# Norm of the mixing input by tokens with x turned on TensorE, a new order around the first gathers, and a gather ring of six slots with one weight unit kept on chip

## The reference, cut to what matters

```python
def layer(x, ret_state, conv_buf, ...):          # x: 1024 prompt frames + 32 sample frames, 1024 wide
    h = rmsnorm(x, g_mix)                        # over each token's 1024 numbers
    q, k, v, g, gb, gc, hc = split(h @ w_in)     # w_in 1024 x 3584: 2048 columns q,k,v,g, then 1536 of the conv
    o = retention(rotary(q), rotary(k), v)       # 4 heads x 128, state carried on from chunk to chunk
    o = rms_scale(o) * silu(g)
    c = gb * short_conv(gc * hc)
    x = x + concat([o, c]) @ w_out
    x = x + peer(rmsnorm(x, g_ffn), wq, keys1, keys2, u_tab, v_tab)
    return rmsnorm(x, g_final)

def peer(x, ...):                                # per token: 8 heads, 16 experts each
    q = (x @ wq).reshape(.., 8, 2, 128)
    ...                                          # top 16 of 128 + 128 keys, top 16 of the 256 pairs
    act = gelu(einsum('td,thkd->thk', x, u_tab[eidx]))
    return einsum('thk,thkd->td', gate * act, v_tab[eidx])
```

## Time and profile before

| | |
|---|---|
| median of 3 runs | 3058.72 us (3057.13 to 3068.32) |
| the profiled execution, its own time | 3063.58 us |
| its span in the trace | 3061.8 us |
| first gather issued | at 135.17 us of the span |
| last gather issued | at 3032.74 us of the span |
| bytes moved by DMA | 1228.73 MB |

### The profile page before, as it was taken

How to read it: one execution, slowest core, us unless ns; L and a number is a source line. 1 busy time by engine, 2 the same in 40 slices (tenths; PEclk the granted TensorE clock), 3 DMA queues, 4 the chain that set the end, 5 groups by cost and what they waited for, 6 DMA issues and landing times.

```text
span 3061.8 us, 36499 instructions
## 1 busy us (share of the span) xinstructions
PE 2305.2 (75%) x12780; PEld 1879.1 (61%) x12780; DVE 2066.9 (68%) x5094; ACT 2035.8 (66%) x3700; POOL 1223.2 (40%) x1060
## 2 busy tenths in 40 slices
PE   8977887787677887877666787888777775667766
PEld 6766677665566775755555666665556555555554
DVE  2365887666688775666888844566578899954454
ACT  1177766667677666776676766667766777676665
POOL 0033333344433333443333344334434444555653
PEclk9988999888888989888888989989987887666666
DMA  7499999999999999999999999999999999999997
GB/s 298 151 377 402 398 420 405 420 420 409 421 418 419 418 416 412 420 411 420 420 417 390 411 414 420 419 419 395 412 420 420 413 412 412 415 418 417 422 419 314
DMA packets 184552, 1228.73 MB, mean 401 GB/s; under 512 B 21169, under 2 KB 26481, under 8 KB 44721
## 3 DMA queue, kind: packets, MB, share of 16 engines
q0 software_dynamic: 152064, 1107.36, 87.9%
q1 hardware_dynamic: 32304, 119.04, 9.9%
HBM read 1221.47 MB, written 4.86 MB: 401 GB/s over the span
## 4 chain that ended last, share of the span: by engine, by line
DMA 40%; PE 21%; DVE 21%; ACT 12%; issue 5%; POOL 1%; SPq 0%; DVEq 0%; ACTq 0%; POOLq 0%
DMA ring<-in_uv,idx 38%; DVE ring L1218 10%; PE expert_sum L952 9%; ACT ring L746 5%; PE mm L798 4%; PE x_ps L860 3%; PE mm L805 2%; ACT weights L742 2%; PE mm L894 2%; POOL ring L577 1%; ACT dots L733 1%; ACT L733 1%; DMA xn_in<-in_xT 1%; DVE pairs_left L1116 1%; DVE pairs_left L1156 1%
## 5 line engine op out<-in xcount | busy, mean ns | idle before, releaser
L577 POOL DMA_INDIRECT ring<-in_uv,idx x1056 | 1223.0, 1158 | 1810.2 <-PE expert_sum L952 1577.6
L952 PE MATMUL expert_sum<-ident_sb,ring 128*128 128x128 f32 x8448 | 1363.6, 316 | 592.2 <-ACT ring L746 590.9
L1218 DVE CUSTOM_DVE_ANT_0 ring<-ring,xn 128x1024 f32<-128x1024 f32 x1056 | 1286.0, 1222 | 740.2 <-DMA ring<-in_uv,idx 732.8
L952 PEld LDWEIGHTS expert_sum<-ident_sb,ring 128*128 128x128 f32 x8448 | 1145.6, 164 | 844.9 <-ACT ring L746 783.6
L746 ACT ACTIVATE ring<-ring,weights 128x1024 f32<-128x1024 f32 x1056 | 1213.0, 1149 | 35.3
L733 ACT ACTIVATE dots<-dots 128x1 f32<-128x1 f32 x1056 | 211.7, 200 | 792.3 <-DVE dots L1218 788.9
L742 ACT ACTIVATE weights<-dots,gate 128x1 f32<-128x1 f32 x1056 | 311.1, 295 | 39.3 <-ACT dots L733 0.4
L798 PE MATMUL mm<-stream,xn_in 128*128 128x256 f32 (+1 forms) x896 | 254.1, 421 | 77.8 <-ACT qkvg L618 61.8
L894 PE MATMUL mm<-turn,stream 128*128 128x256 f32 (+2 forms) x1024 | 276.7, 397 | 0.0
L798 PEld LDWEIGHTS mm<-stream,xn_in 128*128 128x128 f32 (+1 forms) x896 | 164.1, 199 | 117.9 <-ACT qkvg L618 70.6
L805 PE MATMUL mm<-xn_in,stream 128*128 128x256 f32 (+1 forms) x672 | 191.7, 425 | 31.9 <-ACT conv_tmp L609 21.3
(11 more groups left out here) (171 smaller groups left out, 1499.7 us busy)
## 6 DMA issues: line engine op xcount, KB each, us to landing
stream<-in_wq SPq DMA_DIRECT2D x36, 1024.0 KB, 11.7
stream<-in_w_ret SPq DMA_DIRECT2D x26, 1024.0 KB, 9.7
stream<-in_w_conv SPq DMA_DIRECT2D x24, 1024.0 KB, 11.7
ring<-in_uv,idx POOLq DMA_INDIRECT x1056, 12.3
ring<-in_w_ret SPq DMA_DIRECT2D x7, 1024.0 KB, 12.9
w_out_sb<-in_w_out SPq DMA_DIRECT2D x1, 4096.0 KB, 18.6
x<-in_x SPq DMA_DIRECT2D x8, 512.0 KB, 12.2
out_y<-xn SPq DMA_DIRECT2D x8, 512.0 KB, 9.6
```

What stands on the lines that cost most here:

```text
L577: pool.indirect_dma_start(ring[:, g % RING, :], None, uv, bass.IndirectOffsetOnAxis(ap=rows, axis=0)).then_inc(landed[g % RING], 16)
L952: ins = pe.matmul(expert_sum[:, c * P:(c + 1) * P], ring[:, g % RING, D + c * P:D + (c + 1) * P], ident_sb[:, :], is_transpose=True, start ...
L1218: dve.tensor_tensor_reduce(u, u, xn[:, t % 3, :], 1.0, 0.0, ALU.mult, ALU.add, dots[:, g % RING:g % RING + 1]).then_inc(dotted, 1)
```

## The change

**Norm.** `xT` is gone. x is loaded by tokens. ScalarE squares a tile with the sum along the row (`accum_out`) and takes the root of one column, VectorE inverts that column and scales the tile by it in two halves, TensorE turns the tile in eight transposes into `tp`, and VectorE multiplies by `g_mix` on its way into `xn_in`. For tiles 0, 1, 2 and 4 the x that is loaded for the norm stays as the residual; tiles 3, 5, 6, 7 and the sample tile are loaded twice.

**Weights.** The ring has six slots. The eighth "ret" unit stays in `kept`, in the room of the seventh slot, and is loaded once; the seventh comes through `stream`.

**Order at the start.** x of tile 0 is the first load; small constants move ahead of the later weights, cos and sin for tile 1 are loaded at the start (into the place of `state_s`, which is loaded later). ident and g_mix are issued by ScalarE's queue. Before step 0 the projection takes three PSUM banks in turn. Tile 1's units 4 to 7 move behind step 0 (slots 0 to 3), the query pass of head 1 moves behind units 1 to 3, and its choice moves to slot 0, behind step 0 on VectorE.

```diff
-RING = 7
+RING = 6
+KEPT = RET_UNITS - 1
...
-PASSES = [(0, 0, (0,), -130, 4, 0), (0, 1, (0,), -124, 4, 0), (0, 2, (0,), 6, 2, 1), (0, 3, (0,), 22, 2, 1)]
-PASSES += [(0, h, (0, 1), 40 + 14 * (h - 4), 2, 0) for h in range(4, PH)]
+PASSES = [(0, 0, (0,), -130, 4, 0), (0, 1, (0,), -106, 4, 0), (0, 2, (0,), 12, 3, 1), (0, 3, (0,), 22, 2, 1)]
+PASSES += [(0, h, (0, 1), 43 + 14 * (h - 4), 3, 0) for h in range(4, PH)]
...
-            out.append(("ret", u, 1, -118 + 4 * (u - 1) if u else out_at(0) + 9))
+            out.append(("ret", u, 1, [out_at(0) + 9, -118, -114, -110, 0, 1, 2, 3][u]))
...
+def x_turn_at(t):
+    if t < 2:
+        return first_use_at(0) - 4 + 16 * t
+    return first_use_at(group_of(t)) - 10 + 4 * place(t)
...
 def choose_at(h, t):
+    if (h, t) == (1, 0):
+        return 0
...
-            def norm(j):                                         # ScalarE
-                    act.activation(conv_tmp[:, k % 2, 0:w], xn_of_group(j)[:, k, :], ACT.Square).then_inc(squared, 1)
-                act.activation(rstd[:, 0:w], mm[:, 1, 0:w], ACT.Sqrt, bias=eps_sb[:, :],
-                               scale=1.0 / D).then_inc(rooted, 1)
+            def norm(t):
+                yield x_turn_at(t) - 3
+                act.activation(vg_of(t)[0:n, :], x_of(t)[0:n, :], ACT.Square,
+                               accum_out=stat[0:n, 8:9]).then_inc(x_squared, 1)
+                act.activation(stat[0:n, 8:9], stat[0:n, 8:9], ACT.Sqrt, bias=eps_sb[0:n, :],
+                               scale=1.0 / D).then_inc(x_squared, 1)
...
-            def norm(j):                                         # TensorE
-                    pe.matmul(mm[:, 1, 0:w], ones[:, :], conv_tmp[:, k % 2, 0:w], start=(k == 0),
-                              stop=(k == KC - 1)).then_inc(summed, 1)
...
-            def norm(j):                                         # VectorE
-                op(dve.reciprocal(rstd[:, 0:w], rstd[:, 0:w]))
-                for k in range(KC):
-                    dve.scalar_tensor_tensor(xk, xk, g_mix_sb[:, k:k + 1], rstd[:, 0:w],
-                                             ALU.mult, ALU.mult).then_inc(normed, 1)
+            def norm(t):
+                yield x_turn_at(t) - 1
+                op(dve.reciprocal(stat[0:n, 9:10], stat[0:n, 8:9]))
+                for i in range(2):
+                    dve.tensor_scalar(x_hat_of(t)[0:n, cols], x_of(t)[0:n, cols], stat[0:n, 9:10], None,
+                                      ALU.mult).then_inc(x_scaled, 1)
+                for i in range(2):
+                    yield x_turn_at(t) + 2 + i
+                    dve.tensor_tensor(xn_of_group(j)[:, i * 4:(i + 1) * 4, column(t):column(t) + n],
+                                      tp[:, i, :].rearrange("p (h c) -> p h c", h=4)[:, :, 0:n],
+                                      bc(g_mix_sb[:, i * 4:(i + 1) * 4], 2, n), ALU.mult).then_inc(xnT_copied, 1)
```

More of the change, by code:

```diff
@@ L192, in use_at, with bank_index, bank_before, taken_at @@
     return [x[:3] for x in USES[j]].index((kind, unit, t))
+def bank_index(j, q):
+    return q % 3 if j == 0 and USES[0][q][3] < 0 else 0
+def bank_before(j, q):
+    return max((p for p in range(q) if bank_index(j, p) == bank_index(j, q)), default=None)
+def taken_at(slot):
+    kinds = [x[0] in ("ret", "C") for x in USES[0] if x[3] < slot]
+    return sum(kinds), len(kinds) - sum(kinds)
 def taken(j, q):
@@ L602, in projection @@
                         continue
-                    yield slot + 4
+                    yield slot if slot in range(4) else slot + 4
                     act.wait_ge(projected, USES_BEFORE[j] + q + 1)
@@ L723, in _ @@
             programs = started(*[finish(t) for t in range(TILES + 1)],
-                               *[stage(j) for j in range(4) for stage in (norm, projection)],
+                               *[norm(t) for t in RANK], *[projection(j) for j in range(4)],
                                *[stage(t) for t in RANK for stage in (retention, out)],
@@ L757, in item_in @@
                     return ring[:, n, :]
+                if kind == "ret" and n == KEPT:
+                    pe.wait_ge(kept_in, 16)
+                    return kept
                 if kind == "ret" and j == 0:
@@ L782, in projection @@
                 w = width(j)
-                banks = 2 if j == 0 else 1
                 for q, (kind, unit, t, slot) in enumerate(USES[j]):
                     yield slot
-                    if q == 0:
-                        pe.wait_ge(normed, KC * (j + 1))
-                    if q >= banks:
-                        who, count = taken(j, q - banks)
+                    before = bank_before(j, q)
+                    if before is not None:
+                        who, count = taken(j, before)
                         pe.wait_ge(TAKEN[who], count)
+                    elif j:
+                        by_act, by_dve = taken_all(j - 1)
+                        pe.wait_ge(act_took, by_act)
+                        pe.wait_ge(dve_took, by_dve)
+                        pe.wait_ge(query_copied, copied(max(m for m, p in enumerate(PASSES) if p[5] == 1)))
                     bank = bank_of(j, q)
@@ L796, in projection @@
                         for k in range(KC):
-                            yield slot + k // 3
+                            yield slot if slot in range(4) else slot + k // 3
+                            if k in (0, KC // 2):
+                                pe.wait_ge(xnT_copied, 2 * x_turn(t) + 1 + k // (KC // 2))
                             ins = pe.matmul(bank[0:n, 0:UNIT], xnj[:, k, at:at + n], weight[:, k, :],
@@ L800, in projection @@
                     else:
+                        if unit == 0:
+                            pe.wait_ge(xnT_copied, 2 * x_turn(ORDERS[j][-1]) + 2)
                         if unit % 2 == 0:
@@ L928, in _ @@
             programs = started(*[back(t) for t in range(TILES + 1)],
-                               *[stage(j) for j in range(4) for stage in (norm, projection)],
+                               *[projection(j) for j in range(4)],
                                *[stage(t) for t in RANK for stage in (retention, out)],
@@ L1203, in _ @@
             programs = started(*[finish(t) for t in range(TILES + 1)],
-                               *[stage(j) for j in range(4) for stage in (norm, conv)],
+                               *[norm(t) for t in RANK], *[conv(j) for j in range(4)],
                                *[stage(t) for t in RANK for stage in (retention, out)],
```

210 lines of the change are left out of this document (132 added, 78 removed).

## The result

The changed kernel takes 3088.79 us (median of four runs, 3085.11 to 3097.88), the kernel before 3060.34 in the same comparison: ratio 1.0091, interval 1.0069 to 1.0114. It is 28 us slower, where 20 us faster was forecast. The profiled execution took 3097.88 with a span of 3095.9.

The account below looks back on a forecast made before the run. From about 187 us on, bytes over DMA rate plus dry-queue stretches bound the kernel; before that, a chain of dependent work. -19 - 8 - 5 + 12 = -20 gave a median of 3039 us, 8-in-10 range 3020 to 3056.

Parts of the forecast that it names:

- A, the start: Start up to the 13th gather: new norm, loads and order bring it forward, -19 us, bounds -24 and -10.
- the second slow unit: First projection at the start: a second weight unit might also run slow by the clock, shrinking the start's gain by 2 us.
- B, the bytes: Full queue behind the ramp: net 3.41 MB less to move at 0.42 MB a us, -8 us.
- C, the norm's stalls: Norms of groups 1 and 3: waits of the old norm partly go, -5 us, bounds -9 and +3.
- the first stall: Group 1's norm: ScalarE waits 5.02 us for xT and the window behind it loses 2.9 us.
- D, the slot: Gather ring with six slots for seven: the queue runs dry more often, +12 us, bounds +4 and +25.
- The shortfall: Sign in the 50 us windows outside the norms: summed shortfall against 422 GB/s higher by 5 to 15 us.
- Rival 3: Expert-choice stretches: queue runs dry once in each of 22 windows, +55 for +12, net +23, 3082 us; chance 0.07.
- ten windows: 50 us windows from 200 to 3050 whose minimum landing is below 7.9 us; seven of them were counted for the slot's loss.
- The estimate from one transfer alone: Gather ring: 4.4 us a gather without a queue puts the threshold at 6.9 and the slot's cost at about +5.
- the row's: Gather ring: estimate from the least landing seen, 5.4 us, threshold 7.9, giving +12 for the slot.

Follow-up runs that it names:

- experiment 1: The changed kernel with seven ring slots and nothing kept, the eighth unit streamed in every group: 3041.35 us, ratio 0.9933 to the kernel before.
- experiment 3: The changed kernel with six ring slots and nothing kept, the eighth unit streamed in every group: 3097.36 us, ratio 1.0112 to the kernel before.
- experiment 2: The kernel before with six ring slots for seven and the eighth unit kept on chip, all else as it was: 3104.43 us, ratio 1.0129.
- experiments 7 and 8: Gathers alone, all else removed, 7 to 1 in flight; then beside VectorE, ScalarE or TensorE work. Three in flight: 2.50, then 2.80, 2.53, 2.64 us a gather.

## Why the prediction was wrong

**A, the start: right.** -19 was forecast. The 13th tile is taken 20.2 us earlier and its step freed at 171.8 for 191.1, 19.3 earlier. The first unit takes 5.43 us, as it did before, and the next two take 7.07 together: the second slow unit did not come. One reason inside it was wrong. I credited the order with part of these 19; undone, it moves the first step and not the end. The order hands over a gain at step 12 that step 32 takes back: of the -19 about -17 is left at step 32 in experiment 1, and 16 of it without the new order.

**B, the bytes: right as far as it can be told.** 1223.50 MB pass, as forecast. The kept unit saves 4.19 MB against experiment 3, 10.0 us at the rate of the forecast, and measures 8.6 by the medians and 6.4 by the ratios, near the noise.

**C, the norm's stalls: near the small end.** Experiment 1 lies 20.5 below the kernel before, by the medians. It has A (17 at step 32) and a net of 0.26 MB less (0.6), so 3 are left for C, where -5 was forecast. By the spans of the two profiled executions, 3061.8 and 3037.6, it would be 6. The step ends of these two tell where: the head start of experiment 1 is 17.1 us at step 32 and 22.4 at step 64, which is the norm of group 1, for which 2.9 were forecast. Across the norm of group 3 it stays, 23.2 at step 528 and 23.0 at step 624, so the 6.3 us seen lost there did not come back. A deep window stays near the norm of group 1, which had 298 GB/s before; the changed kernel, and below it that of experiment 1:

```profile
260.00:270.00 10.00, 7.15 (x29) 6.30 (x30) 5.18 (x10) 9.63 (x19) 2.48 (x3) 0.58 0.77 302
```
```profile
260.00:270.00 10.00, 10.00 (x53) 8.74 (x52) 4.93 (x8) 9.06 (x19) 4.52 (x4) 0.81 0.91 337
```

ScalarE is busy for 9.63 of the 10 us in the first, and in the second TensorE for all 10 and ScalarE for 9.06: nothing waits for a load any more, the work itself fills the engines. So C is 3 to 6 us, and as far as the step ends tell all of it comes from the first stall; what takes the place of the second stays open.

**D, the slot: the step that failed.** +12 was forecast, 51 to 56 is measured. With the other terms as measured, -17 - 8 - 3 + 56 is the 28 us slower. The mechanism is the one named, a queue that runs dry in the stretches with side work; the term was mis-sized, four to five times too small. The shortfall that was to grow by 5 to 15 us grew by 61, from 38 to 99 us against 420 GB/s. Rival 3's +55 is the number that came, and so is the total: 28 slower, where 23 were worked out for it. Its count, once a window in 22 windows, is not what happened. Two statements of the prediction's part D don't hold:

- "The queue runs dry when a gather's time to landing would fall below 5.4." A landing of 5.4 happens at 356 GB/s. Beside VectorE a full queue needs more than three gathers in flight: three give 2.80 us each and a landing of 8.4, four give 2.49 and 9.7. With a slot less, each gather that now lands within 8.4 + 2.49 = 10.9 falls under the first of these marks. In the trace of before these are 211 of 1020 gathers, not ten windows; with six slots (experiment 2) 143 of 1002 do land within 8.4, for 34 before. The mark of 8.4 is of the worst case, so this is the order of the count and not the count.
- "Each loses at most 2.49 more", one loss a window. A stretch in which the ring is late loses rate at each gather, and there are many in a window. Of the 2800 bins of 1 us from 200 to 3000, 63 are below 330 GB/s before and 183 in the changed kernel, and they lose 27 and 74 us: 47 more.

The number of gathers in flight shows where the loss lies. Issue and landing times of all gathers from 200 to 3000 us give the share of time for each number, and the transfers that start in it the rate (before, and six slots):

| in flight | rates, GB/s | before, share | six slots (experiment 2), share |
|---|---|---|---|
| 0 or 1 | - and 232 | 0.0% | 0.7% |
| 2 | 332 and 343 | 1.5% | 6.9% |
| 3 | 397 and 402 | 9.4% | 27.0% |
| 4 | 414 and 416 | 29.8% | 55.3% |
| 5 and more | 419 and 420 | 59.4% | 10.1% |

Share times (1 - rate/420) times 2800 us, summed, is 38 us before and 91 with six slots: 53 more. Measured are 42.6, and 7.5 for the 3.14 MB less that experiment 2 moves: 50. That these agree is no proof of the table, since the sum over all numbers is only the shortfall of the mean rates, 414 and 406 against 420. What can be set against it are the rates of experiments 7 and 8, which no kernel gave: put in for the table's, they make six slots 36 us slower than seven by the gathers alone, 66 beside TensorE and 107 beside VectorE. The measured 50 lies between, and gathers alone are not enough for it.

**The ring as a sum.** One cycle of a slot is its number of slots times 2.49 when the queue is full. From landing to the next issue of the slot an undisturbed step takes 5.3 us, the median of the steps 920 to 1040 with five, six, seven and eight slots alike (VectorE's operation, ScalarE's gate and scaling, TensorE's eight transposes, the issue's wait). What is left is the time to land: 7.1 with five slots, 9.6 with six, 12.1 with seven, 14.6 with eight; the median landings of these kernels are 8.7, 10.1, 12.3 and 15.0, and in the steps 920 to 1040 they are 8.6, 9.7 (experiment 2), 12.1 and 14.6 (with five the cycle itself is longer). Against the 9.7 of four in flight beside VectorE that leaves seven slots 2.4 us for a step that comes late, and six slots none: each delay by side work costs at once. Five slots must take (5.3 + 8.4)/5 = 2.74 us a step even undisturbed, and the runs show 2.77. That this sum gives the flat late line with six, seven and eight slots, and the step of five, is the strongest support for it; it rests on the run beside VectorE, since by the gathers alone (7.2 with three in flight) five slots would be just enough. It has not been shown which side work causes how much of the delay; the table by stretches only shows that it is all of them.

**The estimate from one transfer alone.** By the Trainium skill, DMA: Bandwidth & Descriptors, section Anatomy of one DMA, a gather alone takes 4.4 us; alone, with one in flight, it lands here after 5.6, counted from the start of an issue that itself takes 0.94, and comes round in 5.84. The estimate of D by it, about +5, was further off than the row's, since it is again the time of one transfer alone and not of one in a full queue.

**The version to take** is the changed kernel with seven slots and nothing kept, 3041.35: 20 us below the kernel before and 47 below the changed one. The old order gives the same (3042.24).

## What to carry to other kernels

Price a buffer of a ring from the distribution of its landings and not from their minimum: measure how many transfers must be in flight for the full rate, with the engines at work that work in the kernel, and count all transfers that would fall below that mark. A ring's depth pays steeply up to (work on a tile + landing at the least number in flight that gives the full rate)/(time of a transfer), here (5.3 + 9.7)/2.49 = 6.0, and one slot above it pays for the delays by side work, here 56 us; a slot more paid 7 to 9. Compare a byte saved with the megabyte that it occupies: the unit kept in 1 MB of room saves 4.2 MB of loads and 6 to 9 us, the same room as ring 56 and as stream buffer 45. And a gain measured some steps into a pipeline may be a loan: look whether it is still there 20 steps on.

## What the runs showed of the hardware

- An indirect gather of 128 rows of 8 KB takes 2.49 us in a full queue (422 GB/s), 2.96 with two in flight and 5.84 alone; three fill the queue when nothing else runs (2.50), but not beside VectorE's two-input operation (2.80) or TensorE's transposes (2.64). Four fill it beside each of them.
- GpSimd's issue of a gather takes 0.94 us, and 1.80 while VectorE runs a two-input operation of 128x1024 at the landing of the gather before. ScalarE's copy and TensorE's transposes leave it at 0.94. In the changed kernel the same issue takes 0.94 at the median, 1.17 us on average and up to 2.57.
- With one or two in flight ScalarE's copy beside the gathers made them no slower (5.68 and 2.88, alone 5.84 and 2.96). Each of these is one execution, and why they came out lower stays open.
